# Routed experts' heads: first rows gathered feature-major in fp32, slot index on GpSimd, first down weights split before the routing

## The chip, the cores and the metric

The kernel runs on one core of a Trainium2 chip. The core has TensorE (PE), VectorE (DVE), ScalarE (ACT), GpSimd (POOL) and SyncE (SP), each with its own instruction queue, and 16 DMA engines. The metric is the device time of one execution in microseconds; lower is better.

## The reference

Four blocks over 256 tokens of width 1024, in fp32: a state-space and attention mixer with a routed feed-forward, a second pair of mixers with a routed feed-forward, a gating mixer with a dense feed-forward, and differential attention with a routed feed-forward. Only the routed feed-forwards matter here. The first kind (two of them) chooses one of 4 groups and 2 of the 4 experts in it:

```
g_p, g_sel = lax.top_k(softmax(t @ w_group + b_group), 1)
top_p, top_i = lax.top_k(softmax(e_logits of the chosen group), 2)
weights = g_p * top_p / sum(top_p)
y = sum over e of gate[:, e] * ((silu(t @ w_gate[e]) * (t @ w_up[e])) @ w_down[e])     # 16 experts, width 256
```

The second kind takes the best 2 of 8 experts of width 3584, weights by a softmax over the two logits.

## The kernel before

The three routed feed-forwards are the phases `m0`, `m1` (4 units, one for each group, each of 4 blocks) and `m2` (8 units, one for each expert, each of 14 blocks). A unit works on up to 128 rows, the tokens that chose it. A block is 256 columns of gate and up and 256 rows of down, 3 MB of weights. Each step of a block multiplies the unit's rows with gate and up, takes silu and product, transposes and multiplies with down. Every fp32 product is made of three fp32r products of halves: a value is cast to `hi` by ACT, and DVE subtracts to get `lo` (one helper, L1856, does all these subtractions, and the products stand at L503, L504, L505). So each step needs six casts of 128x1024 on ACT and six subtractions on DVE. Weights come by SP's queue into two slots; SP issues the load of a gate/up block when the last of the `gu_lo` subtractions of the block before has been done (`gu_split`), and in m0 and m1 also loads the first weight pieces of the next mixer between the first blocks.

Engines are ordered by hand: each engine's program is written out, and semaphores with constant counts join them. The head of a routed phase, on the path from the mixer to the first expert product, goes like this:

- DVE adds the mixer's output and normalizes, tile by tile (two tiles of 128 tokens). PE transposes `h` (L450), ACT copies the features to `xT` (L477; in m2 DVE does it, L470). PE multiplies with the router (L1570), and DVE turns the logits into the chosen group or experts by some 15 to 30 operations of about 0.2 us each (`route_vector`). PE counts ranks (L1579 to L1581). DVE compares `row_index` with `row_of` and writes the 0/1 matrix `pick_t` of token by slot (L1895).
- `keep_busy_tensor` (L444) is filler: fp32 products of 128x128 with no use but to keep PE at work. One call shows as two records.
- The first unit's rows do not come through memory but are gathered by PE. ACT casts `h` (in m2 `normed`) to `tok_hi` (L1749) and DVE subtracts to `tok_lo`; PE multiplies `pick_t` with both (L1524, `gather_tensor`), ACT copies the two halves to `row_x` (L1708), PE transposes (L1536, `rows_turn_tensor`), and ACT and DVE split the result to `xg_hi` (L1713) and `xg_lo`. Later units' rows come by an indirect DMA to `row_x` and take the same transposes.
- DVE then works out the slot index (L2312 to L2327), the flag, the gates from the exponents (L1792 on ACT, behind the mask on DVE), and writes `record` for the scatter by GpSimd (L804). GpSimd's queue has before that two copies of the tokens to memory (L796, L799).
- In the first step of the first unit, `down_hi_scalar` and `down_lo_vector` split the down weights behind the second block's gate and up.

Of the kernel before, what the change touches and what calls it, by code (L numbers as in the profile page):

```python
# [172 lines left out]
def build(nc, w, out):  # L173
# [133 lines left out]
    counts = {"dve": 0, "act": 0}  # L307
# [450 lines left out]

    def scratch_gpsimd(pool):
# [12 lines left out]
    def routed_gpsimd(pool, t):  # L772
# [26 lines left out]
        g.dma_start(by_tile(token_sums), h if t == "m2" else scaled).then_inc(sem("scratch_moved"), 16)  # L799
        pool.wait_ge(sem("route_flag"), 2 * r + 2)  # L800
# [586 lines left out]
    tok_hi, tok_lo = parts("tok_hi", T, D), parts("tok_lo", T, D)  # L1387
    xt_hi, xt_lo = parts_at("xt_hi", tok_at, DC, S), parts_at("xt_lo", tok_at + 4 * DC * S, DC, S)
# [119 lines left out]
    def gather_matmuls():  # L1508
        for c in range(DC):
            for j in range(T):  # L1510
                last = nc.tensor.matmul(psum[5 + c // 4][:, (c % 4) * P:(c % 4 + 1) * P],
                                        ov_rows[:, j, :].rearrange("t (p c) -> t c p", c=DC)[:, c, :],
                                        pick_t[:, j, :].bitcast(F32), start=(j == 0), stop=(j == T - 1))
            if c % 4 == 3:
                yield last

    def gather_tensor(pe, t):

        pe.wait_ge(sem("pick_ready"), 2 * ROUTER[t] + 1)
        for half in range(2):  # L1520
            cols = slice(half * 512, (half + 1) * 512)
            for j in range(T):
                for part, src in enumerate((tok_lo, tok_hi)):
                    last = nc.tensor.matmul(psum[5 + half], pick_t[:, j, :], src[:, j, cols],  # L1524
                                            start=(j == 0 and part == 0), stop=(j == T - 1 and part == 1))
            last.then_inc(sem("gathered"), 1)

    def rows_turn_tensor(pe, t, u):

        for c in range(DC):  # L1530
            if c == 0:
                if isinstance(u, int) and u == 0:
                    pe.wait_ge(sem("row_x_ready"), 2 * ROUTER[t] + 2)
                else:
                    pe.wait_ge(sem("rows_fetched"), 16 * (FFS[t][2] - ROUTER[t] + u))
# [69 lines left out]
    def moe_tensor(pe, t, route):  # L1605
# [74 lines left out]

    def first_weights_scalar(act, t):
# [21 lines left out]

    def row_x_scalar(act, t):

        for half in range(2):
            act.wait_ge(sem("gathered"), 2 * ROUTER[t] + half + 1)
            nc.scalar.copy(row_x[:, half * 512:(half + 1) * 512], psum[5 + half]).then_inc(sem("row_x_ready"), 1)  # L1708
# [25 lines left out]
    def ff_scalar(act, t):  # L1734
# [6 lines left out]
        else:  # L1741
            if t != "m2":
                features_tile_scalar(act, t, 0)
            for j in range(T):
                if t == "m2":
                    act.wait_ge(sem("normed"), j + 1)
                else:
                    tile_wait(act, t, j)
                nc.scalar.copy(tok_hi[:, j, :], (normed if t == "m2" else h)[:, j, :]).then_inc(sem("tok_hi_ready"), 1)  # L1749
            if t != "m2":  # L1750
                features_tile_scalar(act, t, 1)

        def begin(st, following):
# [4 lines left out]
            down_hi_scalar(act, st, 0)  # L1758
            down_hi_scalar(act, st, 1)
        if t == "ff":  # L1760
# [170 lines left out]
    def ff_vector(dve, t):  # L1931
# [74 lines left out]
        down_lo_vector(dve, st, (0, 1))  # L2006
# [113 lines left out]
    def overflow_tensor(pe, t, flag):  # L2120
        n_units, nb = FFS[t][3], FFS[t][4]
        done, dve, act = sem(f"ov_pe_{t}"), sem(f"ov_dve_{t}"), sem(f"ov_act_{t}")
        with pe.If(flag > 0):
            with pe.Fori(0, n_units) as u:
                pe.wait_ge(dve, ov_at("dve", t, u, 0, 4))
                pe.wait_ge(sem(f"ov_load_{t}"), 16)
                for last in gather_matmuls():
# [90 lines left out]
    def tok_lo_vector(dve, t, j):  # L2218

        dve.wait_ge(sem("tok_hi_ready"), T * ROUTER[t] + j + 1)  # L2220
        rest(tok_lo[:, j, :], (normed if t == "m2" else h)[:, j, :], tok_hi[:, j, :]).then_inc(sem("tok_ready"), 1)

# [8 lines left out]
    def route_vector(dve, t, bias):  # L2231
# [41 lines left out]
        if not grouped:  # L2273
            best_two(sem("route_member"))
            exponents()
            tok_lo_vector(dve, t, 1)
# [12 lines left out]
        slot_index_vector(t)  # L2289
# [25 lines left out]
    def slot_index_vector(t):  # L2315

        n = UNITS[t]
        row, ranks, index = (x[:, :, 0:CHOICES[t]] for x in (s_row, s_rank, slot_index))
        if FFR[t]:
            vlink(V.tensor_copy(s_hot[:, :, 0, :], member))  # L2320
        else:
            vlink(V.tensor_copy(s_hot[:, :, 0, :], r_one))
            vlink(V.tensor_tensor(s_hot[:, :, 1, :], member, r_one, ALU.subtract))
        of_choice_vector(t, row_of, row)
# [1077 lines left out]
```

## Time and the profile before

| what | us |
|---|---|
| median of 3 runs (lowest, highest) | 2140.82 (2140.34, 2142.41) |
| the profiled execution, time | 2141.92 |
| the profiled execution, span | 2140.1 |
| first expert product of m0, m1, m2 at | 213.5, 513.5, 1178.3 |

A profile gives, for each engine, what it executed and when, from the span's start. An idle time before an instruction is given with what ended it. The table's last line is the start of the first L503 product behind each head.

### The profile page before, as it was taken

The page shows a single profiled execution, that of the slowest core. Times are in us where ns is not written, and L with a number is a line of the kernel's source. Part 1 is how long each engine was busy: PE and PEld are TensorE (multiplying, and loading weights), DVE is VectorE, ACT ScalarE, POOL GpSimd, SP SyncE. Part 2 cuts the span into 40 slices and gives each one's busy share as a digit, 9 for nine tenths or more (in the row PEclk, how much of TensorE's full clock was granted, in tenths as well). Part 3 has the DMA queues.
Part 4 walks back from the last instruction along what each step waited for, and adds up shares of the span by engine and source line. Part 5 has one row for each costly group of instructions (what it writes and reads, how often), then busy time and mean ns, then how long its engine had stood idle before and what let it go on. Part 6 is the DMA issues. An engine that isn't in the chain of part 4 may idle for free.

```text
span 2140.1 us, 30894 instructions
## 1 busy us (share of the span) xinstructions
PE 2076.6 (97%) x10092; PEld 1699.9 (79%) x10092; DVE 1700.9 (79%) x2276; ACT 1418.4 (66%) x1889; POOL 130.3 (6%) x122
## 2 busy tenths in 40 slices
PE   8999999999998999999999999999999999999998
PEld 7876787867887887887776888888888888888887
DVE  4755998747997657445776999999999999999997
ACT  5662785444784634444442888888888888888885
POOL 1000100001000001111110100000000000000000
PEclk9999999999999999999999999999999999999999
DMA  7317895426993455551342799999999999999995
GB/s 274 135 75 288 338 410 203 163 97 243 412 382 113 183 219 214 200 200 72 137 177 99 316 379 387 371 382 384 368 390 377 385 374 389 374 382 378 366 403 204
DMA packets 88342, 601.59 MB, mean 281 GB/s; under 512 B 10336, under 2 KB 10400, under 8 KB 19776
## 3 DMA queue, kind: packets, MB, share of 16 engines
q1 hardware_dynamic: 79744, 570.40, 67.7%
q0 software_dynamic: 8512, 30.05, 4.7%
q8 instruction: 53, 0.87, 0.2%
q14 instruction: 33, 0.27, 0.0%
HBM read 585.11 MB, written 15.30 MB: 281 GB/s over the span
## 4 chain that ended last, share of the span: by engine, by line
PE 84%; DVE 9%; ACT 2%; DMA 2%; issue 2%; POOL 0%; DVEq 0%; SPq 0%; ACTq 0%
PE bank L503 24%; PE bank L505 24%; PE bank L504 24%; PE bank L1034 2%; PE bank L1494 2%; DVE gu_lo L1856 1%; PE bank L630 1%; DMA ffw_gu<-in_gate_up_m 1%; PE bank L2968 1%; DVE small L395 1%; DVE dn_lo L1856 1%; DMA pieces<-in_pieces 1%; PE bank L1536 1%; DVE pj_lo L540 1%; PE bank L444 0%
## 5 line engine op out<-in xcount | busy, mean ns | idle before, releaser
L1856 DVE TENSOR_TENSOR gu_lo<-ffw_gu,gu_hi 128x1024 fp32r<-128x1024 f32 x620 | 754.7, 1236 | 93.1 <-ACT gu_hi L1671 78.7
L1671 ACT CAST gu_hi<-ffw_gu 128x1024 fp32r<-128x1024 f32 x620 | 649.2, 1052 | 85.1 <-PE bank L505 44.3
L503 PE MATMUL bank<-gu_hi,xg_lo 128*128 128x512 f32 x1152 | 461.3, 400 | 0.0
L505 PE MATMUL bank<-gu_hi,xg_hi 128*128 128x512 f32 x1152 | 450.5, 391 | 0.0
L504 PE MATMUL bank<-gu_lo,xg_hi 128*128 128x512 f32 x1152 | 449.6, 390 | 0.0
L1856 DVE TENSOR_TENSOR dn_lo<-ffw_d,dn_hi 128x1024 fp32r<-128x1024 f32 x299 | 365.5, 1230 | 26.4 <-ACT dn_hi L1679 17.1
L1679 ACT CAST dn_hi<-ffw_d 128x1024 fp32r<-128x1024 f32 x310 | 326.5, 1056 | 63.1 <-PE bank L505 56.0
L503 PE MATMUL bank<-dn_hi,hidt_lo 128*128 128x512 f32 x664 | 260.0, 392 | 6.6 <-DVE hidt_lo L1856 6.4
L505 PE MATMUL bank<-dn_hi,hidt_hi 128*128 128x512 f32 x664 | 258.5, 389 | 0.0
L504 PE MATMUL bank<-dn_lo,hidt_hi 128*128 128x512 f32 x664 | 258.4, 389 | 0.0
L505 PEld LDWEIGHTS bank<-gu_hi,xg_hi 128*128 128x128 f32 x1152 | 216.2, 188 | 45.8
L504 PEld LDWEIGHTS bank<-gu_lo,xg_hi 128*128 128x128 f32 x1152 | 216.9, 188 | 41.1
L503 PEld LDWEIGHTS bank<-gu_hi,xg_lo 128*128 128x128 f32 x1152 | 216.4, 188 | 40.6
L540 DVE TENSOR_TENSOR pj_lo<-pieces,pj_hi 128x1024 fp32r<-128x1024 f32 (+2 forms) x108 | 125.9, 1180 | 63.0 <-ACT pj_hi L530 54.0
L530 ACT CAST pj_hi<-pieces 128x1024 fp32r<-128x1024 f32 (+2 forms) x104 | 103.7, 1012 | 100.2 <-PE bank L505 86.2
L503 PEld LDWEIGHTS bank<-dn_hi,hidt_lo 128*128 128x128 f32 x664 | 124.6, 188 | 35.3 <-DVE hidt_lo L1856 9.1
L1701 ACT CAST hidt_hi<-bank 128x256 fp32r<-128x256 f32 x166 | 61.9, 373 | 127.4 <-PE bank L1494 127.0
L505 PEld LDWEIGHTS bank<-dn_hi,hidt_hi 128*128 128x128 f32 x664 | 124.6, 188 | 26.1
L504 PEld LDWEIGHTS bank<-dn_lo,hidt_hi 128*128 128x128 f32 x664 | 124.7, 188 | 25.4
L503 PE MATMUL bank<-pj_hi,xm_lo 128*128 128x512 f32 (+1 forms) x304 | 124.0, 408 | 11.8 <-DVE xm_lo L485 10.3
L505 PE MATMUL bank<-pj_hi,xm_hi 128*128 128x512 f32 (+1 forms) x304 | 119.5, 393 | 0.0
L504 PE MATMUL bank<-pj_lo,xm_hi 128*128 128x512 f32 (+1 forms) x304 | 119.5, 393 | 0.0
(442 smaller groups left out, 2688.3 us busy)
## 6 DMA issues: line engine op xcount, KB each, us to landing
ffw_gu<-in_gate_up_m SPq DMA_DIRECT2D x288, 1024.0 KB, 7.3
ffw_d<-in_down_m SPq DMA_DIRECT2D x144, 1024.0 KB, 8.9
pieces<-in_pieces SPq DMA_DIRECT2D x70, 1024.0 KB, 7.1
ffw_gu<-in_gate_up_ff SPq DMA_DIRECT2D x22, 1024.0 KB, 7.0
ffw_d<-in_down_ff SPq DMA_DIRECT2D x11, 1024.0 KB, 8.8
h<-token_sums POOLq DMA_DIRECT2D x3, 1024.0 KB, 7.0
pieces<-in_pieces SPq DMA_DIRECT2D x4, 512.0 KB, 8.0
norm_vec<-in_ln_g POOLq DMA_DIRECT2D x4, 512.0 KB, 4.5
```

The source lines that it names most:

```text
L395: vlink(V.bn_stats(out=stats[:, j, k, :], in_=h[:, j, 512 * k:512 * (k + 1)]))
L503: nc.tensor.matmul(bank, a_lo, b_hi, start=start, stop=False)
L504: nc.tensor.matmul(bank, a_hi, b_lo, start=False, stop=False)
L505: return nc.tensor.matmul(bank, a_hi, b_hi, start=False, stop=stop)
L530: nc.scalar.copy(pj_hi[:, 2 * k:2 * k + 2, 0:cols], piece_ap(g)[:, 2 * k:2 * k + 2, :]).then_inc(sem("pj_hi_ready"), 1)
L540: V.tensor_tensor(pj_lo[:, cs, 0:cols], piece_ap(g)[:, cs, :], pj_hi[:, cs, 0:cols].bitcast(F32), ALU.subtract).then_inc(sem("pj_split"), 1)
L1034: last = nc.tensor.matmul(psum[2 * j + half], ev_mixT[:, k, c, TILES[j]], piece_ap(even_out[k])[:, c, half * 512:(half + 1) * 512], start= ...
L1494: last = nc.tensor.transpose(psum[2][:, at:at + P], hid[:, st["par"], f * P:(f + 1) * P], ident)
L1671: nc.scalar.copy(gu_hi[:, 2 * k:2 * k + 2, :], ffw_gu[:, blk["slot"], 2 * k:2 * k + 2, :])\
L1679: nc.scalar.copy(dn_hi[:, f, :], ffw_d[:, blk["slot"], f, :]).then_inc(sem("down_hi_ready"), 1)
L1701: nc.scalar.copy(hidT_hi[:, st["par"]].rearrange("p f t -> p (f t)"), psum[2][:, st["par"] * BLK:(st["par"] + 1) * BLK]).then_inc(sem("hid ...
L1856: return V.tensor_tensor(out, x, hi.bitcast(F32), ALU.subtract)
```

## The change

- The first rows of each routed phase are gathered feature-major: PE multiplies `h` (or `normed`), as the stationary operand in slices of 128 features, with `pick_t` as fp32, and writes the transposed rows into the banks from which `xg_hi` and `xg_lo` are split. `tok_hi`, `tok_lo`, the copies to `row_x` and the eight transposes for the first unit go, and two filler calls with them (4 and 8). PE takes the first pair of feature slices as soon as their split is done.
- The slot index is worked out by GpSimd in `slot_index_gpsimd`, behind the two token copies and ahead of the wait for the flag. In m2, DVE waits for it before it writes the record.
- On ACT the exponent stands behind the split of the rows, with the Exp table loaded ahead of it and the Silu table behind.
- The down weights of the first block are split before the routing: `first_down_scalar` on ACT once the mixer's last product is done, `down_lo_vector` on DVE ahead of the wait for the logits.

```diff
+    def slot_index_gpsimd(pool, t):
+        g, n, choices = nc.gpsimd, UNITS[t], CHOICES[t]
...
+        pool.wait_ge(sem("pick_ready"), 2 * ROUTER[t] + 1)
+        if FFR[t]:
+            glink(g.tensor_copy(s_hot[:, :, 0, :], member))
+        else:
+            glink(g.tensor_copy(s_hot[:, :, 0, :], r_one))
+            glink(g.tensor_tensor(s_hot[:, :, 1, :], member, r_one, ALU.subtract))
+        for values, out in ((row_of, row), (over(rank, 1, T), ranks)):
+            glink(g.tensor_tensor(part, hot, over(values, 2, choices), ALU.mult))
+            glink(g.tensor_tensor(part[:, :, :, 0:4], part[:, :, :, 0:4], part[:, :, :, 4:8], ALU.add))
+            glink(g.tensor_tensor(part[:, :, :, 0:2], part[:, :, :, 0:2], part[:, :, :, 2:4], ALU.add))
+            glink(g.tensor_tensor(out, part[:, :, :, 0], part[:, :, :, 1], ALU.add))
+        glink(g.tensor_scalar(row, row, float(n), None, ALU.mult))
+        glink(g.tensor_tensor(row, row, ranks, ALU.subtract))
+        glink(g.tensor_scalar(index, row, float(8 - n), None, ALU.add), sem("slot_indexed"))
...
     def gather_tensor(pe, t):
         pe.wait_ge(sem("pick_ready"), 2 * ROUTER[t] + 1)
-        for half in range(2):
-            cols = slice(half * 512, (half + 1) * 512)
-            for j in range(T):
-                for part, src in enumerate((tok_lo, tok_hi)):
-                    last = nc.tensor.matmul(psum[5 + half], pick_t[:, j, :], src[:, j, cols],
-                                            start=(j == 0 and part == 0), stop=(j == T - 1 and part == 1))
-            last.then_inc(sem("gathered"), 1)
+        if t == "m2":
+            pe.wait_ge(sem("normed"), T)
+        for last in gather_matmuls(normed if t == "m2" else h):
+            last.then_inc(sem("rows_turned"), 1)
...
-        pe.wait_ge(sem("tok_ready"), T * (ROUTER[t] + 1))
         gather_tensor(pe, t)
-        keep_busy_tensor(1, 4)
-        rows_turn_tensor(pe, t, 0)
-        keep_busy_tensor(1, 8)
-        pe.wait_ge(sem("rows_split"), 2 * q0 + 2)
         st = make_step(t, 0, 0, 0)
         for pair in range(2):
+            pe.wait_ge(sem("rows_split"), 2 * q0 + pair + 1)
             gate_up_tensor(pe, st, x_of(0), pair)
...
+    def first_down_scalar(act, t):
+        mixer = {"m0": "ev", "m1": "od", "m2": "da"}[t]
+        act.wait_ge(sem("out_tile"), T * (MIXER[mixer] + 1))
+        for f in range(2):
+            down_hi_scalar(act, make_step(t, 0, 0, 0), f)
...
             gu_hi_scalar(act, following, (3,))
-            down_hi_scalar(act, st, 0)
-            down_hi_scalar(act, st, 1)
...
+        first_down_scalar(act, t)
         if t != "m2":
-            act.wait_ge(sem("tok_ready"), T * (ROUTER[t] + 1))
             for j in range(T):
+                tile_wait(act, t, j)
                 ins = nc.scalar.activation(scaled[:, j, :], h[:, j, :], ACT.Copy, scale=ALPHA)
             ins.then_inc(sem("h_scaled"), 1)
-        act.wait_ge(sem("route_masked"), ROUTER[t] + 1)
-        nc.scalar.activation(r_e, r_e, ACT.Exp).then_inc(sem("route_exp"), 1)
...
-        row_x_scalar(act, t)
+        nc.scalar.preload_act_table(ACT.Exp)
         rows_hi_scalar(act, q0, 0)
+        act.wait_ge(sem("route_masked"), ROUTER[t] + 1)
+        nc.scalar.activation(r_e, r_e, ACT.Exp).then_inc(sem("route_exp"), 1)
         nc.scalar.preload_act_table(ACT.Silu)
...
         gu_lo_vector(dve, following, (3,))
-        down_lo_vector(dve, st, (0, 1))
         units(dve, t, unit)
...
+        down_lo_vector(dve, make_step(t, 0, 0, 0), (0, 1))
         dve.wait_ge(sem("route_logits"), ROUTER[t] + 1)
...
-        slot_index_vector(t)
         rows_lo_vector(dve, FFS[t][2], 0)
...
         else:
+            V.wait_ge(sem("slot_indexed"), ROUTER[t] + 1)
             of_choice_vector(t, gates[:, :, 0:8], record[:, :, :, 1], sem("route_flag"))
```

## Rows read from the trace of the kernel before

**Rows 1.** The page, part 1: busy time, share of the span and instructions by engine.

```profile
PE 2076.6 (97%) x10092; PEld 1699.9 (79%) x10092; DVE 1700.9 (79%) x2276; ACT 1418.4 (66%) x1889; POOL 130.3 (6%) x122
```

**Rows 2.** Two windows, engines' busy us, granted clock, DMA share, GB/s.

```profile
core 0: us, PE busy (x) PEld busy (x) DVE busy (x) ACT busy (x) POOL busy (x), PEclk, DMA share, GB/s
206.00:214.00 8.00, 6.64 (x46) 5.87 (x45) 5.74 (x29) 3.54 (x6) 0.00 (x0) 1.00 0.52 211
222.00:250.00 28.00, 27.64 (x130) 22.58 (x129) 26.52 (x30) 21.65 (x27) 2.73 (x2) 1.00 0.98 395
```

**Rows 3.** Timeline of PE in m0: start, length, instruction, records, idle before.

```profile
203.20 1.81 PE L444 MATMUL bank<-upto,ident 128*128 128x128 f32 x14
...
206.66 0.47 PE L1524 MATMUL bank<-tok_lo,pick_t 128*128 128x512 f32 x1 [0.26 <-DVE pick_t L1895]
...
210.73 1.16 PE L1536 MATMUL bank<-ident,arena 128*128 128x128 f32 x8 [1.10 <-ACT arena L1708]
...
213.52 0.50 PE L503 MATMUL bank<-gu_hi,xg_lo 128*128 128x512 f32 x1
...
225.82 0.50 PE L503 MATMUL bank<-dn_hi,hidt_lo 128*128 128x512 f32 x1 [0.36 <-DVE hidt_lo L1856]
...
253.39 0.50 PE L503 MATMUL bank<-dn_hi,hidt_lo 128*128 128x512 f32 x1 [1.14 <-DVE hidt_lo L1856]
```

**Rows 4.** Timeline of DVE in m0's head.

```profile
199.48 2.36 DVE L1856 TENSOR_TENSOR tok_lo<-h,tok_hi 128x1024 fp32r<-128x1024 f32 x2 [0.25 <-DVE h L417]
...
203.47 0.20 DVE L2246 TENSOR_TENSOR small<-bank,par_all 128x40 f32<-128x40 f32 x1 [1.47 <-PE bank L1570]
...
206.08 0.43 DVE L1895 TENSOR_TENSOR pick_t<-row_index,small 128x256 fp32r<-128x256 f32 x1
...
212.17 1.29 DVE L1856 TENSOR_TENSOR xg_lo<-bank,xg_hi 128x512 fp32r<-128x512 f32 x2 [1.22 <-ACT xg_hi L1713]
...
216.00 0.17 DVE L2331 COPY record<-small 128x8 f32<-128x8 f32 x1
...
219.07 1.23 DVE L1856 TENSOR_TENSOR gu_lo<-ffw_gu,gu_hi 128x1024 fp32r<-128x1024 f32 x1 [0.19 <-ACT gu_hi L1671]
```

**Rows 5.** Timeline of ACT in m0's head.

```profile
200.28 1.06 ACT L477 COPY xT<-bank 128x512 f32<-128x512 f32 x2
...
211.48 1.07 ACT L1713 CAST xg_hi<-bank 128x512 fp32r<-128x512 f32 x2 [0.81 <-PE bank L1536]
212.57 1.28 ACT L1831 ACT_TABLE_LOAD   x1
```

**Rows 6.** The chain that ended last, 185 to 260: start, length, what.

```profile
222.02 2.27 DVE dn_lo L1856 x2
...
237.33 13.26 DMA ffw_gu<-in_gate_up_m
```

**Rows 7.** SP's queue: the first load of m0's fourth block.

```profile
222.05 0.80 SPq L2017 DMA_DIRECT2D ffw_gu<-in_gate_up_m  x2
```

**Rows 8.** Timelines of PE and of DVE in m2's head.

```profile
1170.93 1.36 PE L444 MATMUL bank<-upto,ident 128*128 128x128 f32 x10
...
1178.27 0.50 PE L503 MATMUL bank<-gu_hi,xg_lo 128*128 128x512 f32 x1
...
1190.64 0.49 PE L503 MATMUL bank<-dn_hi,hidt_lo 128*128 128x512 f32 x1 [0.44 <-DVE hidt_lo L1856]
...
1167.45 0.17 DVE L2257 TENSOR_TENSOR small<-bank,small 128x16 f32<-128x16 f32 x1
...
1170.81 1.23 DVE L1856 TENSOR_TENSOR tok_lo<-arena,tok_hi 128x1024 fp32r<-128x1024 f32 x1
...
1180.20 0.19 DVE L2313 TENSOR_REDUCE record<-small 128x4 f32<-128x32 f32 x1
```

**Rows 9.** GpSimd's groups by line: shapes, count, busy us, mean ns, idle.

```profile
L1843 POOL TENSOR_TENSOR dn_lo<-ffw_d,dn_hi 128x1024 fp32r<-128x1024 f32 x11 | 26.4, 2396 | 145.2 <-ACT dn_hi L1679 145.1
...
L376 POOL TENSOR_TENSOR small<-small 128x1 f32<-128x1 f32 x18 | 10.2, 567 | 482.9 <-DVEq L381 482.9
```

**Rows 10.** DVE's groups in the dense phase, 860 to 1000.

```profile
L1856 DVE TENSOR_TENSOR gu_lo<-ffw_gu,gu_hi 128x1024 fp32r<-128x1024 f32 x32 | 45.8, 1449 | 12.0 <-ACT gu_hi L1671 12.0
```

More of the change, by code:

```diff
@@ L304, in piece_wait @@
         eng.wait_ge(sem(f"piece_landed{n % PSLOTS}"), 32 * (n // PSLOTS + n % PSLOTS))
-    counts = {"dve": 0, "act": 0}
+    counts = {"dve": 0, "pool": 0}
     def vlink(ins, *also):
@@ L757, in setup_gpsimd, with glink @@
         last.then_inc(sem("const_filled"), 1)
+    def glink(ins, *also):
+        counts["pool"] += 1
+        ins.then_inc(sem("pool_step"), 1)
+        nc.gpsimd.wait_ge(sem("pool_step"), counts["pool"])
+        for s in also:
+            nc.gpsimd.sem_inc(s, 1)
+    def slot_index_gpsimd(pool, t):
+        g, n, choices = nc.gpsimd, UNITS[t], CHOICES[t]
+        row, ranks, index = (x[:, :, 0:choices] for x in (s_row, s_rank, slot_index))
+        hot = s_hot[:, :, 0:choices, :]
+        part = s_part[:, :, 0:choices, :]
+        pool.wait_ge(sem("pick_ready"), 2 * ROUTER[t] + 1)
[12 more added lines that the diff above has]
+        glink(g.tensor_scalar(index, row, float(8 - n), None, ALU.add), sem("slot_indexed"))
     def scratch_gpsimd(pool):
@@ L799, in routed_gpsimd @@
         g.dma_start(by_tile(token_sums), h if t == "m2" else scaled).then_inc(sem("scratch_moved"), 16)
+        slot_index_gpsimd(pool, t)
         pool.wait_ge(sem("route_flag"), 2 * r + 2)
@@ L1386, in build @@
     tok_at = arena_at + 4 * carved[0]
-    tok_hi, tok_lo = parts("tok_hi", T, D), parts("tok_lo", T, D)
-    xt_hi, xt_lo = parts_at("xt_hi", tok_at, DC, S), parts_at("xt_lo", tok_at + 4 * DC * S, DC, S)
+    xt_hi, xt_lo = parts("xt_hi", DC, S), parts("xt_lo", DC, S)
     silu_buf = plain(2 * BLK).rearrange("p (a b) -> p a b", a=2)
@@ L1506, in down_tensor, with gather_matmuls @@
             last.then_inc(sem("down_piece"), 1)
-    def gather_matmuls():
+    def gather_matmuls(rows):
         for c in range(DC):
@@ L1511, in gather_matmuls @@
                 last = nc.tensor.matmul(psum[5 + c // 4][:, (c % 4) * P:(c % 4 + 1) * P],
-                                        ov_rows[:, j, :].rearrange("t (p c) -> t c p", c=DC)[:, c, :],
+                                        rows[:, j, :].rearrange("t (p c) -> t c p", c=DC)[:, c, :],
                                         pick_t[:, j, :].bitcast(F32), start=(j == 0), stop=(j == T - 1))
@@ L1531, in rows_turn_tensor @@
             if c == 0:
[L1532 to L1535, printed above, removed]
+                pe.wait_ge(sem("rows_fetched"), 16 * (FFS[t][2] - ROUTER[t] + u))
             last = nc.tensor.transpose(psum[5 + c // 4][:, (c % 4) * P:(c % 4 + 1) * P],
@@ L1702, in hidt_hi_scalar @@
                        psum[2][:, st["par"] * BLK:(st["par"] + 1) * BLK]).then_inc(sem("hidt_hi_ready"), 1)
[L1704 to L1708, printed above, removed]
     def rows_hi_scalar(act, q, side):
@@ L1742, in ff_scalar @@
             if t != "m2":
[L1743 to L1751, printed above, removed]
+                for j in range(T):
+                    features_tile_scalar(act, t, j)
         def begin(st, following):
@@ L2126, in overflow_tensor @@
                 pe.wait_ge(sem(f"ov_load_{t}"), 16)
-                for last in gather_matmuls():
+                for last in gather_matmuls(ov_rows):
                     pass
@@ L2216, in build @@
     s_row, s_rank = tiny(T, 2), tiny(T, 2)
-    def tok_lo_vector(dve, t, j):
-        dve.wait_ge(sem("tok_hi_ready"), T * ROUTER[t] + j + 1)
-        rest(tok_lo[:, j, :], (normed if t == "m2" else h)[:, j, :], tok_hi[:, j, :]).then_inc(sem("tok_ready"), 1)
     def first_max(vals, n, value, onehot, *done):
@@ L2275, in route_vector @@
             exponents()
-            tok_lo_vector(dve, t, 1)
         dve.wait_ge(sem("route_rows"), 2 * ROUTER[t] + 1)
@@ L2313, in of_choice_vector @@
         vlink(V.tensor_reduce(out=out, in_=part, axis=AX, op=ALU.add), *done)
[L2315 to L2324, printed above, removed]
-        of_choice_vector(t, over(rank, 1, T), ranks)
-        vlink(V.scalar_tensor_tensor(out=row, in0=row, scalar=float(n), in1=ranks, op0=ALU.mult, op1=ALU.subtract))
-        vlink(V.tensor_scalar(index, row, float(8 - n), None, ALU.add))
     def slot_gates_vector(t):
@@ L2345, in routed_tiles_vector @@
         dve.sem_inc(sem("phase_done"), 1)
-        for j in range(T):
-            tok_lo_vector(dve, t, j)
     def moe_first_vector(dve, t, i):
@@ L2869, in moe_second_vector @@
         features_tile_vector("m2", 1, gain, sem("xt_tile"))
-        tok_lo_vector(dve, "m2", 0)
         normed_tile_vector(1)
```

## The prediction

> **What bounds the kernel now.** I read the page first: TensorE (PE) is busy 97% of the span and carries 84% of the chain that ended last [rows 1]. So only time in which PE waits, or runs filler, can be won. The change touches the heads of the three routed phases (m0, m1, m2), from the router's logits to the first expert products. The timelines by engine show them. In m0 the head is a relay: the pick matrix is ready (L1895), gather (L1524), two copies on ScalarE (L1708), eight transposes (L1536), split into hi and lo, first product at 213.52 [rows 3, 4, 5]. From 206.51 to 213.52 PE does nothing that the result needs except the gather and the transposes; the rest is filler (L444) or idle. The m1 head repeats m0's, 300.0 us later, to within some hundredths. The m2 head is shorter in copies and waits for one more split on VectorE [rows 8]. Last I asked what follows each head: after m0's, PE stands still once more, 1.14 us at 253.39, behind a weight block whose transfer took 13.26 us, in a stretch where the DMA engines are 98% busy [rows 2, 3, 6]. m1 has the same wait at its own 553.65, of 1.40.
>
> **m0's pick, later.** Two casts and two `tok_lo` splits go (1.05 and 1.2 us each). ScalarE, free of the cast before them, ends the feature copies at about 201.05, where it was 201.34 [rows 5]; it then casts the two down halves, 1.00 each. VectorE used to end `tok_lo` at 201.84 and wait 1.47 for the logits until 203.47 [rows 4]. It now waits for the first down cast (202.05), does two `dn_lo` splits, 2.27 to the start of what follows [rows 6], and starts the logits at about 204.4: +0.9 (+1.2 if the copies do not move). Cover gone here: the 1.47 idle is not enough. The pick matrix, and with it the gather, thus comes at 207.56, was 206.66.
>
> **The gather itself.** Eight 512-column products and eight transposes go; sixteen fp32 128x128 products come, strided `h` as weights, the pick matrix moving. The old trace has the same shape in the filler: one filler call is two records, 14 records last 1.81 us and 10 last 1.36 [rows 3, 8], so 0.1125 a record plus 0.24 tail. 32 records: PE free after 3.60, first half visible after 16 x 0.1125 + 0.23 = 2.03, second after 3.83. The weights of the transposes have the same stride and 8 records take 1.16 [rows 3]. Bounds: below, 3.60; above, 8 records in 1.16 as the pace, 4.64.
>
> **m0's first product.** From 207.56: first half at 209.59, then as before 0.05 to ScalarE, 0.69 from `xg_hi` to `xg_lo` and 0.65 for one half of the 1.29 split: 210.98. PE is free at 211.16. The first product moves from 213.52 to 211.16, so 2.36 won; the second pair needs the second half at 212.8, PE comes there at 211.16 + 2.8 = 213.9.
>
> **What VectorE gives back.** Second half visible 211.39, split done 212.77, was 213.46. Slot index is gone from before it, but VectorE waited 1.22 there anyway [rows 4], so its seven operations (about 1.4 us) are worth nothing in m0. Gates then end at 215.5, was 216.17. The exponent follows the rows at 212.2 and VectorE wants it at 213.2. The Silu table load (1.28) [rows 5] then ends 213.5, and the first `gu_hi` is done 1.05 later, 214.55; `gu_lo` starts at 215.55, so that is hidden by the gates. Three `gu_lo`, gate, hidden and the fourth follow in the old spacing; the third, at 219.07 before, starts at 217.8: VectorE is 1.25 ahead, PE 2.36. PE needs the first `gu_lo` at 211.16 + 5.93 = 217.1 and it is there at 216.75. The 2.27 of `dn_lo` and the two `dn_hi` are gone from this place [rows 6], and with them PE's 0.36 wait [rows 3]: PE is 2.7 ahead.
>
> **Where it is capped.** The fourth weight block is issued when the last of these `gu_lo` is done (222.05, now 220.8) [rows 7]. From there the DMA engines run without a gap up to the block landing at 250.6 [rows 2, 6]. With the same bytes at the same rate it lands 1.25 earlier, and so PE restarts at 253.39 - 1.25 = 252.1, though by its own work it would be there at 252.25 - 2.7 = 249.6: the wait grows from 1.1 to 2.6. m0 is worth 1.25, m1 the same. Were the 13.26 a delay from the issue and not a queue, each would be worth 2.7.
>
> **m2.** Before the member flags VectorE loses one `tok_lo` and gains the two `dn_lo`: +1.13 on the logits of 1167.45. The other `tok_lo` (1170.81, 1.23) stood right before the pick and goes. The pick stays where it was, near 1172.7. But PE's ten filler records start after the rank products, so at 1172.06 instead of 1170.93, and hold PE until 1173.19. PE is free at 1176.79 and `rows_split` comes at 1173.19 + 2.03 + 0.05 + 0.69 + 0.65 = 1176.61. First product 1176.8, was 1178.27: 1.48. With the 0.44 of `hidt_lo` [rows 8] 1.9. No piece transfers follow here, and PE has no wait until the end: nothing caps it.
>
> **Slot index on GpSimd.** 12 operations in m0 and m1 (a copy, twice four, three at the end), 13 in m2, each waiting for the one before; the wait for the pick is behind the two token DMAs on the queue, issued by then. In m0 and m1 only the scatter waits for them, due at 215.5; in m2 VectorE waits too, ahead of all its `gu_lo`. It used to reach these gates of the record at 1179.97, two operations of which the last is at 1180.20 [rows 8]; the rows' split ended just before the product that waited for it, 1178.27, and now ends at 1173.19 + 3.83 + 0.05 + 0.69 + 0.65 = 1178.41, so it asks at 1180.2, the pick is ready at 1172.75: 7.4 us, 0.57 an operation; PE has 0.9 of patience behind that, so 0.64. Bounds: the cheapest two-input row is 128x1 at 0.57, by power; by the 128x1024 split, 2.4 us, an element is 2.3 ns at most [rows 9], so near nothing for 32 elements; with 0.1 to 0.3 between dependent ones, 0.2 to 0.85 each, 2.6 to 11 us in all. I take 0.45: hidden. At the upper end PE stops some 2.8 us. These operations also run beside VectorE. With GpSimd splitting in the dense phase, `gu_lo` means 1.45 us, not 1.23 [rows 4, 10]: the two slow each other. Here VectorE's work is small operations and a split that reads PSUM, and GpSimd is mostly done before the gates; between nothing and, by that ratio (0.22 in 1.23) on the 2.8 us of gates, 0.5 a head; I take nothing.
> The Trainium skill (GPSIMD Engine Reference, section 1, Specifications) says that both share SBUF interfaces, and that VectorE instructions with two SBUF inputs contend; the dense phase's rows agree, 1.45 against 1.23. By its section 3.1, 2.6 cycles an element at 1.2 GHz, 32 elements would be 0.07 us, an estimate, and the sum would not change.
>
> **Sum.** 1.25 + 1.25 + 1.9 = 4.4 us. The profiled execution took 2141.92 (span 2140.1 and 1.8 around it), so 2137.5; the median of the runs lies 1.1 lower, 2140.82, so 2136.4. About 0.2% is what a measurement of this kernel can tell from no change, 4.3 us: the forecast lies on that line.
>
> **Rivals.**
> One, no cap: the transfer is not a full queue, or frees sooner. 2.7 + 2.7 + 1.9 = 7.3: 2133.5. For it: issues come earlier too. Against: 395 GB/s and 98% [rows 2], the same as where nothing waits. Chance 0.17.
> Two, the new wait in m2 and the contention: GpSimd needs over 0.64 an operation, or each head loses 0.5 to slower small operations. At 0.85, 4.4 - 2.8 = 1.6: 2139.2. For it: dependent operations in a row on GpSimd never occur before. Against: memsets and iotas there are short. The gather at 0.145 a record (+1.04 a head) gives 4.4 - 3.1 = 1.3, the same place. Chance 0.25.
> Three, on the other side: the fp32 gather costs four records a product, or strided weights are not hidden, so 7.2 us a head: +3.6 each, against 4.4 won: 6.4 slower, 2147.2. It decides from 1.5 us a head on. Against: the filler is fp32 too and shows two records [rows 3]. Chance 0.08.
> A falling TensorE clock I leave out: the new idle is about 0.9 before the rank products in m0 and 1.5 in m2, and the stretch with 1.36 of idle was granted 1.00 [rows 2].
>
> **Numbers.** Forecast 2136.4 with chance 0.5, its own range 2134.8 to 2138 (cap 1 to 1.8 a head). The range reaches to the cap-free case and to the second: 2133.5 to 2140.5. Faster by over 0.2%: rival one and a bit over half of the forecast's case, 0.47; within: 0.44; slower: 0.09.
>
> **What would show it.** After: logits operation of m0 near 204.4; gather of 32 records in 3.8; m0's first product at 211.2, and that of m2 1.5 earlier against its own last projection; no wait at 225.8; the wait at 253 grown from 1.1 to about 2.5 and the block landed 1.25 earlier; VectorE in m2 without a wait on GpSimd. Wrong, if that wait is long, if a gather record is over 0.12, or if the 253 wait did not grow.

## The result, and the profile after

The changed kernel takes 2151.42 us in the median of 6 runs (2146.32 to 2152.73), where the kernel before took 2141.18 beside it (2140.34 to 2142.41, 6 runs). The ratio is 1.0041, 95% interval 1.0031 to 1.0051. It is slower by about 10 us where 4.4 were to be won, and lies outside the range. The profiled execution took 2149.56, with a span of 2147.8, 7.7 more than before's; it is 1.9 below the median of its six, so the tables below hold somewhat less than the whole loss.

The page, part 1, answers to [rows 1]: VectorE is busy for 10.8 us less, as the change meant, but TensorE for 8.2 more.

```profile
PE 2084.8 (97%) x10068; PEld 1709.7 (80%) x10068; DVE 1690.1 (79%) x2248; ACT 1411.6 (66%) x1879; POOL 140.9 (7%) x159
```

PE's timeline in m0 and, behind the second dots, m2 answers to [rows 3, 8].

```profile
197.21 4.02 PE L444 MATMUL bank<-upto,ident 128*128 128x128 f32 x20
...
207.42 0.40 PE L1602 MATMUL bank<-small,upto 128*128 128x16 f32 x2 [0.97 <-DVEq L315]
...
209.19 7.88 PE L1540 MATMUL bank<-pick_t,h 128*128 128x128 f32 x32 [0.16 <-DVE pick_t L1906]
216.82 0.47 PE L503 MATMUL bank<-gu_hi,xg_lo 128*128 128x512 f32 x1
...
243.29 1.16 PE L1559 MATMUL bank<-ident,arena 128*128 128x128 f32 x8 [0.45 <-DMA arena<-token_rows,slots]
...
257.30 0.50 PE L503 MATMUL bank<-dn_hi,hidt_lo 128*128 128x512 f32 x1 [1.69 <-DVE hidt_lo L1867]
...
1179.16 7.78 PE L1540 MATMUL bank<-pick_t,arena 128*128 128x128 f32 x32
1186.69 0.48 PE L503 MATMUL bank<-gu_hi,xg_lo 128*128 128x512 f32 x1
```

The gather has the 32 records that were expected, but they take 7.88 us, not 3.8. Without the tail of 0.24 that is 0.24 a record, where the filler beside it keeps 0.1125. It isn't a missing record or a wait: all 32 are there, and the group has no idle time in it. DVE's timeline in the same head shows who waits for it (an answer to [rows 4]).

```profile
203.84 2.36 DVE L1867 TENSOR_TENSOR dn_lo<-ffw_d,dn_hi 128x1024 fp32r<-128x1024 f32 x2 [3.54 <-ACT dn_hi L1698]
206.11 0.19 DVE L2252 TENSOR_TENSOR small<-bank,par_all 128x40 f32<-128x40 f32 x1
...
208.71 0.42 DVE L1906 TENSOR_TENSOR pick_t<-row_index,small 128x256 fp32r<-128x256 f32 x1
...
213.91 0.69 DVE L1867 TENSOR_TENSOR xg_lo<-bank,xg_hi 128x512 fp32r<-128x512 f32 x1 [1.89 <-ACT xg_hi L1733]
217.73 0.69 DVE L1867 TENSOR_TENSOR xg_lo<-bank,xg_hi 128x512 fp32r<-128x512 f32 x1 [3.13 <-ACT xg_hi L1733]
```

Where the time is, for all kernels that follow, in two lengths: a head, from the first transpose (L450) of a phase's input to its first expert product, split at the start of the gather; and the units, from that product to the last transposes of a pick matrix. Microseconds of the profiled executions:

| kernel | m0 head | m1 head | m2 head | units m0, m1, m2 |
|---|---|---|---|---|
| before | 13.69 + 6.86 | 13.68 + 6.86 | 17.97 + 5.55 | 134.36, 134.61, 944.22 |
| after | 15.64 + 7.63 | 14.96 + 7.64 | 18.52 + 7.53 | 135.18, 135.36, 943.47 |
| only the gather | 13.42 + 7.64 | 13.77 + 7.64 | 18.73 + 7.54 | 136.01, 135.73, 944.83 |
| after, contiguous | 15.63 + 3.73 | 15.99 + 3.73 | 18.53 + 3.49 | 135.00, 135.46, 944.41 |
| the same, down split late | 14.45 + 3.72 | 14.81 + 3.73 | 16.76 + 3.50 | 135.55, 138.44, 945.80 |

From before to after the heads grow by 7.3 us and the units by 0.8; the span grew by 7.7. So the loss is in the heads: 3.5 from the gather on, 3.8 ahead of it. Of the 3.8 the prediction had 2.3 itself (the pick 0.9 later in m0 and m1, and the gather 0.47 later in m2).

### The profile page after: what moved, and what is told of

Read it like the earlier page. It is cut to its first block, busy times and chain, and to the rows that moved or that the text cites. A ratio compares the mean times of both kernels' runs of the same rounds, so it can differ in the third digit from the quotient of the medians.

```text
span 2147.8 us, 30847 instructions
## 1 busy us (share of the span) xinstructions
PE 2084.8 (97%) x10068; PEld 1709.7 (80%) x10068; DVE 1690.1 (79%) x2248; ACT 1411.6 (66%) x1879; POOL 140.9 (7%) x159
## 4 chain that ended last, share of the span: by engine, by line
PE 85%; DVE 8%; ACT 2%; DMA 2%; issue 2%; POOL 1%; DVEq 0%; SPq 0%; ACTq 0%; POOLq 0%
PE bank L503 24%; PE bank L505 24%; PE bank L504 24%; PE bank L1064 2%; PE bank L1523 2%; PE bank L630 1%; PE bank L2956 1%; PE bank L1540 1%; DVE pj_lo L540 1%; DVE small L395 1%; DMA ffw_gu<-in_gate_up_m 1%; DMA pieces<-in_pieces 1%; DVE gu_lo L1867 1%; PE bank L1559 1%; DMA arena<-token_rows,slots 1%
```

## Experiments

Medians of before beside these runs are 2141.85 (21 runs) for experiments 1 to 4, 2141.82 (29 runs) for 5 to 8, and 2141.51 (13 runs) for 9 and 10.

**1. The stride alone.** The changed kernel, with neighbouring features as the stationary operand, and gate and up weights laid out to match:

```diff
-    rows[:, j, :].rearrange("t (p c) -> t c p", c=DC)[:, c, :],
+    rows[:, j, c * P:(c + 1) * P],
...
-    row_x.rearrange("t (p c) -> t c p", c=DC)[:, c, :], ident)
+    row_x[:, c * P:(c + 1) * P], ident)
...
+    if chunked:
+        parts = [m.reshape(e, DC, P, n // BLK, BLK).transpose(0, 3, 2, 1, 4) for m in (gate, up)]
```

> The changed kernel, with the weights of the gather (and of the later transposes) as contiguous slices of 128 features, and the gate and up weights laid out to match; nothing else moves, instruction for instruction. Theory one: the gather's records are long (0.243 us instead of the filler's 0.112) because its weight loads are strided by 8 elements in a plain fp32 product (336 ns in the trace after, 192 for the filler's). Then a record takes 0.11 to 0.13 us, the gather 3.6 to 4.0, and the time falls by about 4 us a head below the changed kernel, to 2136 to 2139. Theory two: the records are long because each brings new weights, or because the pick matrix is the moving operand; then a record stays near 0.24 and the time at 2149 to 2152. Theory three: the loss is in the clock, which fell in the head of m0 after; then the time stays above 2145 although the gather is short.

Measured: 2138.89 (2136.48 to 2141.37, 11 runs), ratio 0.9989 [0.998, 0.9998]. That is 12.5 under the changed kernel and 3.0 under before. Its timeline of PE in m0:

```profile
206.69 3.84 PE L1540 MATMUL bank<-pick_t,h 128*128 128x128 f32 x32 [0.17 <-DVE pick_t L1906]
210.42 0.50 PE L503 MATMUL bank<-gu_hi,xg_lo 128*128 128x512 f32 x1
```

The instructions of the pick tile, by form, in the changed kernel: count, shortest, median and longest in ns.

```profile
L1540 PEld LDWEIGHTS bank<-pick_t,h x64: 312/336/337, 209.2 to 520.0; 128*128 128x128 f32 x64
L1540 PE MATMUL bank<-pick_t,h x64: 400/402/504, 209.2 to 520.1; 128*128 128x128 f32 x64
```

and in this one:

```profile
L1540 PEld LDWEIGHTS bank<-pick_t,h x64: 186/192/192, 206.7 to 509.8; 128*128 128x128 f32 x64
L1540 PE MATMUL bank<-pick_t,h x64: 275/275/377, 206.7 to 509.9; 128*128 128x128 f32 x64
```

Same count of records, same shapes, same operands: only the weight load is longer, 336 ns against 192, and the product with it. The edit also makes the transposes of later units contiguous (their load goes from 192 to 140 ns in the median), but by the table the units gain no more than 0.2 us by it in m0 and nothing in m1 and m2.

**2. The gather alone.** The kernel before with the changed gather (strided), everything else as it was.

```diff
-        for half in range(2):
...
-                    last = nc.tensor.matmul(psum[5 + half], pick_t[:, j, :], src[:, j, cols],
...
+        if t == "m2":
+            pe.wait_ge(sem("normed"), T)
+        for last in gather_matmuls(normed if t == "m2" else h):
+            last.then_inc(sem("rows_turned"), 1)
```

> The kernel before, with the new strided gather alone: casts, splits, copies and the first transposes gone, slot index, exponent and down split where they were. Theory one: in m0 and m1 the gather starts where it did (206.7), PE is free 7.6 later, the second half's split ends at about 215.9 instead of 213.5, and VectorE and with it the transfers are 2.4 later; in m2 the pick comes two splits earlier and about 0.5 is lost. Sum 2141.2 + 5.3, 2145 to 2148. If the early down split and GpSimd's index were what costs, 2137 to 2141.

Measured: 2150.74 (2147.99 to 2153.96, 5 runs), ratio 1.0044 [1.0031, 1.0058]. This one part is as slow as the whole change, and slower than expected (2145 to 2148); its gather takes 7.89. In its profile the heads are 5.1 us longer than before's and the units 3.4.

**3. The down split back in the first step,** otherwise experiment 1.

```diff
-        first_down_scalar(act, t)
-        down_lo_vector(dve, make_step(t, 0, 0, 0), (0, 1))
...
+            down_hi_scalar(act, st, 0)
+            down_hi_scalar(act, st, 1)
...
+        down_lo_vector(dve, st, (0, 1))
```

> As e1_contiguous, with the first down weights split in the first step as before. Theory one, with the early split a loss on the path of the logits: logits in m0 at 203.4, first product at 210.3, VectorE 1.5 ahead of the kernel before; in m2 the pick is 1.7 earlier and the first product 3.5 to 4 earlier. 2133 to 2136. If the early split is worth its price (PE's waits of 0.36 and 0.44 gone), this is no faster than e1_contiguous, 2136 to 2139.

Measured: 2137.71 (2133.95 to 2140.38, 11 runs), ratio 0.998 [0.9971, 0.9989]; 1.2 under experiment 1, by less than the noise, since the two intervals overlap. The heads are 1.2, 1.2 and 1.8 shorter. In return a wait that the early split had removed is there, in m0 and with 1.41 in m1:

```profile
222.41 0.50 PE L503 MATMUL bank<-dn_hi,hidt_lo 128*128 128x512 f32 x1 [1.40 <-DVE hidt_lo L1868]
```

So in m0 and m1 the early split moves about as much as it saves. In m1, TensorE also waits 2.59 us for the next unit's rows, and the units there are 3.0 longer.

**4. A probe of the stride.** The changed kernel with 128 more products at the end of PE's queue, their results unused: sixteen fp32 products at each stride of 1, 2, 4 and 8 elements of the stationary operand, sixteen fp32r products at 1 and 8, sixteen transposes at 1 and 8. An fp32 product shows as two records, each of the other two kinds as one.

```diff
+    for stride in (1, 2, 4, 8):
+        wts = pieces[:, 0, 0:P * stride].rearrange("t (p c) -> t c p", c=stride)[:, 0, :]
+        for _ in range(16):
+            nc.tensor.matmul(psum[0][:, 0:P], wts, ident, start=True, stop=True)
```

> The changed kernel with PE alone given 128 more products at the end of its queue, results unused: sixteen each of plain fp32 with weights at strides 1, 2, 4 and 8 elements and the identity moving; of fp32r at strides 1 and 8; of transposes with data at strides 1 and 8. Theory one: fp32 loads take 192 ns at stride 1 and 336 at stride 8, records 0.11 and 0.24 us; transposes stay near 0.12 at either stride, as in the trace before. Open is where the price sets in, and whether fp32r weights pay it too. Theory two (the pick matrix or new weights): all strides alike.

Measured: 2179.74, one run. Weight loads by line and form, in one window within each stride (so the counts are those of the window), in this order: fp32 at 1, 2, 4 and 8 (L3309), fp32r at 1 and 8 (L3314), transposes at 1 and 8 (L3318). The last number is the mean in ns.

```profile
L3309 PEld LDWEIGHTS bank<-ident,pieces 128*128 128x128 f32 x27 | 3.1, 192 | 0.0
L3309 PEld LDWEIGHTS bank<-ident,pieces 128*128 128x128 f32 x27 | 3.3, 196 | 0.0
L3309 PEld LDWEIGHTS bank<-ident,pieces 128*128 128x128 f32 x14 | 3.4, 330 | 0.0
L3309 PEld LDWEIGHTS bank<-ident,pieces 128*128 128x128 f32 x29 | 7.0, 335 | 0.0
L3314 PEld LDWEIGHTS bank<-gu_lo,gu_hi 128*128 128x128 f32 x14 | 1.6, 192 | 0.0
L3314 PEld LDWEIGHTS bank<-gu_lo,gu_hi 128*128 128x128 f32 x12 | 3.0, 337 | 0.0
L3318 PEld LDWEIGHTS bank<-ident,pieces 128*128 128x128 f32 x16 | 1.8, 143 | 0.0
L3318 PEld LDWEIGHTS bank<-ident,pieces 128*128 128x128 f32 x15 | 1.7, 187 | 0.0
```

Two elements (8 bytes) are free, four (16 bytes) cost the full price, eight cost no more. fp32r pays like fp32. A transpose pays 44 ns of load, and its pace stays at 0.11 a record (all 32 take 3.68 us).

**5. The early down split alone,** in the kernel before.

```diff
+        first_down_scalar(act, t)
+        down_lo_vector(dve, make_step(t, 0, 0, 0), (0, 1))
...
-            down_hi_scalar(act, st, 0)
-            down_hi_scalar(act, st, 1)
-        down_lo_vector(dve, st, (0, 1))
```

> The kernel before, with the first down weights split ahead of the routing and nothing else. If the early split is a loss on the path of the logits: in m0 and m1 it follows the two splits of the old gather, the logits are read about 1.2 later and the first product moves from 20.5 after the head's first transpose to 21.7; the units get 0.4 shorter; in m2 the head grows by 2.3 and the units shrink by 0.4. Sum +3.5 to +4.5 on 2141.9, 2145 to 2146.5. If it only moves work that waited anyway, 2141 to 2142.

Measured: 2150.81 (2147.62 to 2151.54, 5 runs), ratio 1.0043 [1.003, 1.0056], more than the 2145 to 2146.5 expected. The heads of m0 and m1 are 1.2 and 1.4 longer, that of m2 6.4. VectorE's timeline in m2 shows why:

```profile
1169.18 2.36 DVE L1862 TENSOR_TENSOR dn_lo<-ffw_d,dn_hi 128x1024 fp32r<-128x1024 f32 x2 [1.94 <-ACT dn_hi L1679]
1171.46 0.17 DVE L2263 TENSOR_TENSOR small<-bank,small 128x16 f32<-128x16 f32 x1
```

In this order ScalarE's two down casts stand behind the cast of `tok_hi` for the second tile, VectorE waits 1.94 for them, splits, and only then takes the logits, at 1171.46 instead of 1167.45 [rows 8]. PE stood idle 4.53 before its rank products, and its clock fell to 1.2 GHz behind that, which the window (the last three numbers are clock, DMA share, GB/s) puts at 0.50. Of the 6.4, 4.0 are the late logits. The changed kernel has no cast of `tok_hi` to stand behind, and there m2's way to the gather is 0.55 longer than before's; what the early split costs in it is read from experiments 1 and 3.

```profile
1174.00:1180.50 6.50, 6.25 (x23) 5.68 (x24) 3.91 (x16) 0.81 (x2) 0.00 (x0) 0.50 0.03 11
```

**6. Only the slot index on GpSimd and the exponent behind the rows,** in the kernel before.

```diff
-        slot_index_vector(t)
+        slot_index_gpsimd(pool, t)
...
-        act.wait_ge(sem("route_masked"), ROUTER[t] + 1)
-        nc.scalar.activation(r_e, r_e, ACT.Exp).then_inc(sem("route_exp"), 1)
         row_x_scalar(act, t)
         rows_hi_scalar(act, q0, 0)
+        act.wait_ge(sem("route_masked"), ROUTER[t] + 1)
+        nc.scalar.activation(r_e, r_e, ACT.Exp).then_inc(sem("route_exp"), 1)
```

> The kernel before, with the slot index on GpSimd and the exponent behind the rows, and nothing else; the old gather stays. If the index is free and the exponent had held up the copies of the rows in m0 and m1 (0.6 each): 0 to 0.7 shorter heads in m0 and m1, nothing in m2 (VectorE waited 2.3 there), 2139.5 to 2142. If GpSimd slows VectorE's small operations or m2 waits for it, 2143 or more.

Measured: 2138.83 (2137.74 to 2143.31, 11 runs), ratio 0.9989 [0.998, 0.9997]. From the gather on, the heads of m0 and m1 take 5.48 us instead of 6.86: ScalarE's copies of the gathered rows had stood behind the exponent, and that had waited 4.31 for its input in the kernel before. This is more than the 0 to 0.7 expected, and the median lies under the expected 2139.5. In m2 nothing moves.

**7. The transfers that were to be the cap.** Experiment 3 with the next layer's pieces loaded between blocks 8 and 11, not 0 and 3.

```diff
-        for i in range(2 if t in NEXT else 0):
+        early = 0 if t not in NEXT else 2 if t == "ff" else 6
+        for i in range(early):
...
+                if i >= early - 2:
+                    load_piece_half(sp, early_pieces + i - early + 2, c)
```

> As e3_contiguous_late_down, with the next mixer's first two weight pieces loaded between the blocks 8 to 11 of m0 and m1 and not between the blocks 0 to 3. If the transfers cap what the head wins, as predicted: PE's waits behind blocks and rows in the first 50 us of m0 and m1 (2.7 us in m0 of e3_contiguous_late_down) shrink below 1, and 1 to 2 us are won in each, 2133.5 to 2136.5 against 2137.7. If the waits have another cause, no change, 2137 to 2138.5.

Measured: 2143.97 (2139.3 to 2150.23, 12 runs), ratio 1.001 [1.0, 1.002]: worse than its parent by 6. The wait for the next unit's rows stayed in m0 (1.36, in the parent 1.29), though the pieces no longer load beside them; in m1 the parent's 2.59 is gone, but it is gone in the parent's twin too (experiment 10). ScalarE's waits from 262 to 345, in this kernel and then in its parent (us in total, times, longest):

```profile
ACT gu_hi L1690 <- DMA ffw_gu<-in_gate_up_m: 10.6, 6, 3.6
```

```profile
ACT gu_hi L1690 <- DMA ffw_gu<-in_gate_up_m: 3.1, 4, 1.3
```

The pieces only hurt later, where weight blocks are due at once: three new waits of PE in that stretch of m0, 3.2 us in all, and as much in m1. Neither expectation came true, and the cap at 253 stays undecided by it.

**8. The contiguous gather alone,** in the kernel before (experiment 2 with the slices of experiment 1).

> The kernel before, with the new gather alone and its weights contiguous; index, exponent and down split where they were. If stride is the whole cost of the gather: 12 us below e2_only_gather, 2138 to 2139. VectorE's index now stands ahead of the split of the rows, so in m0 and m1 the first product is about 1.2 later than in e3_contiguous_late_down. If the index on GpSimd and the late exponent earn nothing, 2137.5, the same as e3_contiguous_late_down; if they earn their 1.2 in two heads, 2138.5 to 2140.

Measured: 2139.38 (2135.31 to 2142.93, 11 runs), ratio 0.9989 [0.998, 0.9998]. That is 11.4 under experiment 2: the stride costs as much in this surrounding as in the changed kernel. From the gather on the heads of m0 and m1 take 5.16 and 5.17, 1.4 longer than in experiment 3: VectorE's slot index stands ahead of the split of the rows, and PE waits 1.32 for that split before the first product.

**9 and 10. What gives the lead back.** In m0 of the kernel before, GpSimd's timeline has the list of slots read, and the rows of the next unit fetched by it; SP's first load of the fourth block [rows 7] comes after the first of the two.

```profile
221.24 0.58 POOL L807 DMA_DIRECT2D slots<-slot_table_m  x1 [1.41 <-DMA slot_table_m<-record,slot_index]
223.38 1.78 POOL L784 DMA_INDIRECT arena<-token_rows,slots  x1 [1.56 <-DMA slots<-slot_table_m]
```

In the changed kernel the same list, on GpSimd's queue, and that load, on SP's, come in the other order, as they do in experiments 1 and 3:

```profile
227.04 0.58 POOL L837 DMA_DIRECT2D slots<-slot_table_m  x1 [1.42 <-DMA slot_table_m<-record,slot_index]
233.22 1.69 POOL L813 DMA_INDIRECT arena<-token_rows,slots  x1 [5.60 <-DMA slots<-slot_table_m]
...
226.53 0.80 SPq L2027 DMA_DIRECT2D ffw_gu<-in_gate_up_m  x2
```

The wait for a 16 KB list is 5.60 instead of 1.56, and PE then waits for the rows. So experiment 9 starts that chain earlier: experiment 3 with the table of m0 and m1 written from a constant record, without VectorE's gates (it leaves out the gates of the later units). Number 10 is experiment 3 again, as its twin.

```diff
-        pool.wait_ge(sem("route_flag"), 2 * r + 2)
+        if t == "m2":
+            pool.wait_ge(sem("route_flag"), 2 * r + 2)
...
-    in_=record[:, j, c, :], in_offset=None)
+    in_=record[:, j, c, :] if t == "m2" else listing[:, j, :], in_offset=None)
```

> The version with contiguous slices and the down split in the first step, in which m0's and m1's table of slots is scattered from a constant record (token numbers, no gates), so that GpSimd does not wait for VectorE's gates. It leaves out the gates of the units behind the first in m0 and m1 (they are zero in the table). In the twin the slot index is ready at 508.50, the scatter starts at 513.34, the fetch of the next unit's rows at 524.65, and TensorE stands still for them, 1.29 us in m0 and 2.59 in m1. Theory one, the chain of record, table, list and fetch sets this wait, and it is not the saturated weight stream: the scatter starts at about 508.6, the fetch 3 to 5 us earlier, both waits are gone and do not come back at hidt_lo; the time is 2 to 4 us under the twin's. Theory two, the capped weight stream: the waits for rows go, but a wait for hidt_lo of 1 to 3 us takes their place within the next block, and the time is within 1 us of the twin's.

> The same kernel as the third experiment (contiguous slices, down split in the first step), run again beside the early table as its twin: 2137.7, as before, 3.5 to 4.5 us under the kernel before, with waits for the rows of the second unit of 1 to 3 us in m0 and m1.

Measured: 2135.34 (2133.82 to 2138.63, 7 runs), ratio 0.9971 [0.996, 0.9982], and for the twin 2136.26 (2135.03 to 2142.38, 7 runs), 0.9976 [0.9965, 0.9987]. GpSimd and PE in m1, in experiment 9:

```profile
508.64 1.12 POOL L838 DMA_INDIRECT slot_table_m<-listing,slot_index  x1 [0.82 <-POOL slot_index L789]
...
512.46 0.59 POOL L842 DMA_DIRECT2D slots<-slot_table_m  x1 [1.41 <-DMA slot_table_m<-listing,slot_index]
514.65 1.02 POOL L816 DMA_INDIRECT arena<-token_rows,slots  x1 [1.61 <-DMA slots<-slot_table_m]
```

and in the twin, with PE's two waits, m0's for rows and m1's, which in this execution is one behind the weight block and not, as expected, for rows:

```profile
514.64 2.02 POOL L834 DMA_INDIRECT slot_table_m<-record,slot_index  x1 [4.81 <-DVEq L315]
...
525.90 1.00 POOL L813 DMA_INDIRECT arena<-token_rows,slots  x1 [5.12 <-DMA slots<-slot_table_m]
...
238.39 1.09 PE L1559 MATMUL bank<-ident,arena 128*128 128x128 f32 x8 [1.53 <-DMA arena<-token_rows,slots]
...
551.16 0.50 PE L503 MATMUL bank<-dn_hi,hidt_lo 128*128 128x512 f32 x1 [1.30 <-DVE hidt_lo L1868]
```

In experiment 9 both are gone, and nothing takes their place: the units of m0 and m1 last 134.15 and 134.04, in the twin 135.76 and 135.60. In m0, SP issues the fourth block's load 26.7 us behind the head's first transpose, in the twin 27.7, of which the slower clock of its head has 1.0 (see the last section). So the two differ in the chain of the list and not in when the weights are asked for. The mechanism of theory one holds, 1.6 us a phase. Its total does not: 2 to 4 us were expected, the medians differ by 0.9, and their intervals overlap.

## Why the prediction was wrong

**The gather itself: the step that failed.** It priced 32 records at the filler's 0.1125, whose weights are contiguous, and took the transposes of 8 records in 1.16 [rows 3] as proof that the stride is hidden. Both rows were read correctly; neither is the new operation. A transpose keeps its pace at a stride of 32 bytes, a plain product doesn't: 336 ns of load against 192, and 0.24 a record. The trace of before held a sign: its strided transposes (L1536) load in 193 ns in the median, its contiguous ones (L1543) in 138. Beside the filler's 192 the 193 looks like no price. The bound above, 4.64, came from the same transposes and so was no bound. Experiment 1 takes the stride away, with all else in place, and gives back 12.5 us; by the table the part from gather to first product shrinks by 3.9, 3.9 and 4.0, 11.8 in all. Experiment 2 puts the strided gather alone into the kernel before and has the whole loss; experiment 8 takes the stride out of that and gives back 11.4.

Of rival three the half "strided weights are not hidden" happened, in place and kind; its 7.2 a head were 7.88, 7.88 and 7.78. The count of records was two a product, as the filler said. It had a chance of 0.08, which was too little: the filler that was set against it answers only its other half.

The Trainium skill (Advanced Engine Details and Errata, Memory Cachelines) says that SBUF is read in 16-byte lines and that at least two hits on a line are needed for full speed. The probe agrees: stride 2 in fp32, two hits a line, loads in 196 ns, stride 4, one hit, in 330. The prediction had not weighed that rule. That lines are the mechanism is the Trainium skill's word; the runs show the step between 8 and 16 bytes.

**The rest of the change,** tested by experiment 1, was forecast 4.4 us ahead of before and measured 3.0 (by its interval between 0.4 and 4.3), so that the shortfall is hardly clear of noise.
- From gather to first product: forecast 3.60 in m0; measured 3.73. The first product of m2 comes 1.50 earlier than before, counted from the head's first transpose; forecast 1.48. The 0.44 behind it isn't seen in m2's units (944.41 against 944.22).
- The logits behind the down split: forecast 0.9 late. Against before, the changed kernel's gather starts 1.28 later in m1 and 0.55 in m2; m0's 1.95 has the slower clock in it. The measured heads with the early split are 1.2, 1.2 and 1.8 longer than without (experiments 1 and 3), PE idle 0.97 before its rank products in m0 and 1.50 in m2, as forecast. The removal of the wait at 225.8 came true, but it was worth more than 0.36: with the lead of the new gather that wait is 1.40 (experiment 3).
- The slot index on GpSimd: twelve operations in m0, of which these are the first and the last in GpSimd's timeline, a start every 0.29 us where 0.45 was assumed. In m2 it was ready at 1182.45 and VectorE came for it at 1190.0. Hidden, as forecast. VectorE's small operations beside it take 0.16 to 0.17 us, as before, so both halves of rival two are out; and a gather record takes more than its 0.145. That taking the index off VectorE is "worth nothing in m0" was wrong, though: with the new gather, VectorE's wait in which it was hidden is gone, and left on VectorE it costs 1.4 in m0 and m1 (experiment 8).

```profile
209.20 0.19 POOL L775 COPY small<-small 128x16 f32<-128x16 f32 x1 [1.61 <-DVE pick_t L1906]
...
212.41 0.23 POOL L786 TENSOR_SCALAR slot_index<-small 128x2 int32<-128x2 f32 x1
```

- TensorE's clock, put at nothing: in the profiled executions it fell in the head of m0 in the changed kernel, and in those of m0 and m1 in experiments 1 and 3, for about 1.0 us each (see the last section).
- Gates and the exponent behind the rows: no new wait, right. That the old exponent held ScalarE's copies back by 1.4 us in m0 and m1 (experiment 6) had not been priced; the direct gather wins it in any case.

**Where it is capped: right that it is, the cause only in part.** The lead was to be lost to the weight block that lands at 250.6, in a full stream of bytes. In the changed kernel the wait for it is 1.69, in experiment 1 1.88: grown from 1.14, if not to 2.6. But experiment 9 has no wait at the block at all, not even the 1.14 of before, with the DMA engines 100% busy from 222 to 250. Counted from the head's first transpose, PE is there 3.4 us earlier at the first product of m0 than in the kernel before, and still 2.4 earlier behind the wait of 1.41 that the late down split brings. The block's load takes 13.26 us from issue to landing before [rows 6] and 14.53 in the changed kernel; in experiment 9 it is issued at 235.35 and ScalarE works on it from 246.00, 10.65 later. (Experiment 3 and its twin have no wait at the block in m0 either; there PE has already waited, 1.29 and 1.53, for the rows.) What changes is that the small list and the rows are asked for before the fourth block's loads. So a full stream does not make the wait by itself; a chain from record to table to list to rows has a part in it. That is rival one's outcome (no cap), but not its reason, since the queue is full. Two things moved together: the list is waited for 1.56 and not 5.60, and the rows themselves are fetched at 217.06, where the DMA engines stand at 4%, and not inside the full stretch. How much of the wait at 250 is the one and how much the other was not separated, and the test was made with the late down split, not in the changed kernel itself.

**Sum.** Forecast 4.4 won; the part that isn't stride won 3.0 (1.4 less); the stride cost 12.5. 2141.18 - 3.0 + 12.5 = 2150.7, measured 2151.42. The 12.5 is itself the measured distance from experiment 1 to the changed kernel, so this closes by construction but for 0.7 between two medians of before. What stands apart from it are the 11.8 us that the heads give back, and 3 x 4.1 by the pace (32 records at 0.24, not 0.1125).

**A better version.** Experiment 3 and its twin beat both kernels: contiguous slices, slot index on GpSimd, exponent behind the rows, down weights split in the first step, at 0.998 and 0.9976 of before. Whether they are faster than experiment 1, 6 or 8 (0.9989 each) the intervals leave open.

## What to carry to other kernels

Price an operation by a row that shares every property that the engine touches: shape, type, and the stride of each operand. A row that agrees in the stride but is another kind of operation (here a transpose) answers for its kind alone, and where no row has both, the upper bound is not known and the chance of the bad case is not small.

When a stage gets shorter, list what it had been issued ahead of: here the split work came forward, and the weight loads behind it overtook a 16 KB list on which the next unit's rows depend.

## What the runs showed of the hardware

- The weight load of a plain 128x128 fp32 product takes 192 to 196 ns up to 8 bytes between elements and 330 to 336 at 16 and 32 bytes. In fp32r it takes 192 at 4 bytes and 337 at 32 (experiment 4).
- GpSimd waits 5.60 us for a list of 16 KB that is read behind weight loads (changed kernel, m0), 1.56 for one read ahead of them (before, m0); in m1 of experiments 10 and 9, 5.12 and 1.61.
- Dependent GpSimd operations of 2 to 32 elements a partition take 0.19 to 0.26 us each, and start every 0.29 to 0.30.
- TensorE's clock falls within heads where the profiled execution of before shows no fall, and not each time that the same TensorE instructions run. The twin's m1 and experiment 9's run the same 20 filler records, behind the same 0.72 us of idle, in 3.93 and 2.48 us. Windows of PE's busy time, with the granted clock third from the end, for the twin and for experiment 9:

```profile
495.00:499.00 4.00, 4.00 (x22) 4.00 (x23) 2.80 (x5) 0.00 (x0) 1.24 (x3) 0.57 0.00 0
```

```profile
494.00:498.00 4.00, 3.67 (x33) 3.48 (x33) 2.82 (x5) 0.25 (x1) 1.21 (x3) 1.00 0.00 0
```

One is mostly at 1.2 GHz, the other at 2.4 throughout. It makes a head 1.0 longer, as it did ahead of the gather in m0 of the changed kernel (20 records in 4.02, at the top), so single heads can be compared to 1 us only with this column beside them. Of the 3.8 us lost ahead of the gathers it has about 1.0: experiment 1's m1, with the slow clock, takes 15.99 to the gather, the same code in the changed kernel, without it, 14.96. What decides whether it falls stays open.
